# Mixture-of-experts stage: values gathered token by token and weighed in four 32-column groups

## The chip, the cores and the metric

The kernel runs on one core of a Trainium2 chip. The metric is the device time in microseconds (us), here the median of three runs.

## The reference, cut to what matters

One decoder layer, for 1024 prompt tokens and 32 sample tokens. The change touches only its channel mixer, `peer`, in which every token picks 16 of 16384 experts in each of 8 heads (128 slots a token), and every expert is a key row and a value row of 1024 float32 (4 KB each):

```
def block(xb):                                   # 128 tokens
    q = (xb @ w_pq).reshape(PEER_BLOCK, PEER_HEADS, 2, HALF_KEY)
    s = einsum('thpd,pnd->thpn', q, sub_keys)
    sv, si = top_k(s, TOPK)                      # 16 of 128, twice a head
    comb, cidx = sums and numbers of all 256 pairs
    tv, ti = top_k(comb, TOPK)
    eidx = take_along_axis(cidx, ti, axis=-1)
    g = softmax(tv, axis=-1)
    ue, ve = exp_u[eidx], exp_v[eidx]
    a = gelu(einsum('td,thkd->thk', xb, ue))
    return einsum('thk,thkd->td', g * a, ve)
```

## The kernel before, in words

`program` (L1964) runs stage after stage: attention and convolution for both groups of tokens, `merge`, the output product, then `key_weights` (L1378), `experts` (L1486) and the last product. Every stage is a block in which each engine runs its own instruction stream in order, and semaphores alone tie the streams together. All data is float32, and `hT` keeps the residual in SBUF, 128 channels by tokens.

`experts` goes through 8 tiles of 128 prompt tokens and a last tile of the 32 sample tokens, which is folded four times over the 128 partitions, so that it has 2 heads and not 8. A unit is one head of one tile: 66 units. The work of a unit:

- TensorE `score` (L1574): 8 matmuls of 128x256 give the scores of both halves of a key; ScalarE `take_scores` (L1646) copies them to SBUF.
- VectorE `pick` (L1709 to L1754): top 16 of each half, 70 candidate sums, top 16 of these, and the 16 expert numbers (a loop of 16 small operations, L1750). ScalarE `gates` (L1651) takes the exponentials.
- GpSimd `head` (L1536): a copy of the unit's 16 numbers (L1538), then 16 indirect gathers of keys and 16 of values (both L1545). A gather brings one row of 4 KB to each of the 128 partitions, that is for one slot of all 128 tokens, into a ring of 8 buffers `U` or 8 buffers `V`. From the ninth on, a gather waits until its buffer is free.
- VectorE `dot` (L1794, the dot products at L1798): token times key row, one operation a gather, which frees the U buffer.
- ScalarE `weights` (L1657): Gelu of the 16 dots (L1659); VectorE multiplies with the gate (L1802); ScalarE builds for each slot a diagonal matrix of the 128 weights (L1665, ring of 4).
- TensorE `weigh` (L1583): diagonal times V buffer, two matmuls of 128x512 a gather (L1589), added up in PSUM over all slots of the tile. This frees the V buffer.

Picks run a whole tile ahead: `pick` of tile t+1 is interleaved with the dots of tile t, and `advance_indices` (L1756) and `advance` (L1768) pass the finished tile on. So VectorE does 8 picks, then a ninth, before the first dot. In the steady loop VectorE's order is pick(n+8), dot(n); TensorE's is score(n+9), weigh(n); GpSimd's is keys of n, values of n. The loops are hardware loops (`Fori`), and `hold` (L72) is a wait followed by an increment of a counter that nothing reads.

```
L1821-1822  pick(PH * t + PH + h, h)
            dot(PH * t + h, ds(h * TOPK, TOPK))
L1620-1621  score(t + 1, PH * t + PH + h + 1, h + 1)
            weigh(PH * t + h)
```

One other place matters for comparison: sample attention's weighing (L999) runs its matmuls on 32 columns each, four column groups in turn.

Of the kernel before, what the change touches and what calls it, by code (L numbers as in the profile page):

```python
# [7 lines left out]
I32 = mybir.dt.int32  # L8
# [4 lines left out]
ds = bass.ds  # L13
# [1472 lines left out]
def experts(nc, sh, io, wk):  # L1486
    NU, NV, ND = 8, 8, 4
    U0, V0, G0 = NU, NV + TOPK, 1
    NC_ = 70

    blocks = [(0, 2, 16), (2, 8, 5), (8, 16, 1)]
    with Scope(nc, "exp") as s:
        ust = s.sb("ust", [P, KD, P])
        xbn, xb = s.sb("x_next", [P, D]), s.sb("x", [P, D])
        sc = s.sb("scores", [P, 2 * PH, P])
        s1, s2 = s.sb("s1", [P, 2, P]), s.sb("s2", [P, 2, P])
# [4 lines left out]
        tv, ti, tif, ntv = s.sb("tv", [P, TOPK]), s.sb("ti", [P, TOPK], U32), s.sb("tif", [P, TOPK]), s.sb("ntv", [P, 1])  # L1501
        picked, ef = s.sb("picked", [P, TOPK, NC_]), s.sb("ef", [P, TOPK])
        idx_next, idx_cur = s.sb("idx_next", [P, SLOTS], I32), s.sb("idx_cur", [P, SLOTS], I32)
        idx_now = s.sb("idx_now", [P, 2, TOPK], I32)
        ge, gsum, grec, gate = s.sb("ge", [P, SLOTS]), s.sb("gsum", [P, PH]), s.sb("grec", [P, PH]), s.sb("gate", [P, SLOTS])
        dots, act_dots, wt = s.sb("dots", [P, TOPK]), s.sb("act_dots", [P, TOPK]), s.sb("wt", [P, TOPK])
        U, V = s.sb("U", [P, NU, D]), s.sb("V", [P, NV, D])
        diag = s.sb("diag", [P, ND, P])
        fold = s.sb("fold", [P, P])
        ysb = s.sb("y", [P, D])  # L1510
        scb = s.ps("sc")
        xt = [s.ps(f"x{i}") for i in range(2)]
        yb = [s.ps(f"y{i}") for i in range(2)]
        names = ("stage_loaded sc_ready sc_copied xb_turned xb_copied tv_ready gate_done "
                 "idx_ready advanced staged u_free v_free gelu_done w_ready diag_ready y_ready y_copied y_turned y_added "
                 "chain adv iota_made fold_zeroed fold_made passed_p passed_a passed_v passed_t passed_s")
# [3 lines left out]
        HS = SLOTS // REP // TOPK  # L1520

        @block.sync
        def _(sp):
            sp.dma_start(ust[:, :, :], sh.u_s[0]).then_inc(e["stage_loaded"], 16)
            with sp.Fori(1, NT + 1) as t:
                hold(sp, e["sc_ready"], PH * t, e["passed_s"])
                hold(sp, e["xb_turned"], 2 * t, e["passed_s"])
                sp.dma_start(ust[:, :, :], sh.u_s[ds(t, 1)].rearrange("a p m n -> p (a m) n")).then_inc(e["stage_loaded"], 16)

        @block.gpsimd  # L1530
        def _(pool):
            pool.iota(iota[:, :], [[1, NC_]], base=0, channel_multiplier=0, allow_small_or_imprecise_dtypes=True)\
                .then_inc(e["iota_made"], 1)
            pool.memset(fold[:, :], 0.0).then_inc(e["fold_zeroed"], 1)

            def head(n, col, hh):  # L1536
                hold(pool, e["v_free"], V0 + TOPK * (n - 1), e["passed_p"])
                pool.tensor_copy(idx_now[:, hh, :], idx_cur[:, col]).then_inc(e["staged"], 1)  # L1538
                hold(pool, e["staged"], n + 1, e["passed_p"])
                for table, buf, ring, free, first, size in ((io["exp_u"], U, u_in, e["u_free"], U0, NU),  # L1540
                                                            (io["exp_v"], V, v_in, e["v_free"], V0, NV)):
                    for k in range(TOPK):
                        if k % 2 == 0:
                            hold(pool, free, TOPK * n + k + 1 + first - size + 1, e["passed_p"])
                        pool.indirect_dma_start(buf[:, k % size, :], None, table[0],  # L1545
                                                bass.IndirectOffsetOnAxis(idx_now[:, hh, k:k + 1], 0))\
                            .then_inc(ring[k % size], 16)
            with pool.Fori(0, NT) as t:
                hold(pool, e["idx_ready"], t + 1, e["passed_p"])
                with pool.Fori(0, PH // 2) as h2:  # L1550
                    for hh in range(2):
                        head(PH * t + 2 * h2 + hh, ds((2 * h2 + hh) * TOPK, TOPK), hh)
            pool.wait_ge(e["idx_ready"], NT + 1)
            for hh in range(HS):
                head(PH * NT + hh, slice(hh * TOPK, (hh + 1) * TOPK), hh % 2)

        @block.tensor
        def _(pe):
            pe.sem_inc(e["v_free"], V0)
            pe.sem_inc(e["y_copied"], 1)  # L1560
            pe.sem_inc(e["y_turned"], 2)
            pe.sem_inc(e["y_added"], 2)
            pe.sem_inc(e["sc_copied"], 1)

            def turn_tokens(t):

                pe.wait_ge(e["stage_loaded"], 16 * t + 16)
                pe.wait_ge(e["y_added"], 2 if isinstance(t, int) and t == 0 else 2 * t)
# [5 lines left out]
            def score(t, q, h):  # L1574

                pe.wait_ge(e["stage_loaded"], 16 * t + 16)
                pe.wait_ge(e["sc_copied"], q + 1)
                for k in range(KD):
                    last = pe.matmul(scb[:, 0:2 * P].rearrange("p (a n) -> p a n", n=P), ust[:, k, :], wk[:, k, ds(2 * h, 2), :],  # L1579
                                     start=k == 0, stop=k == KD - 1)  # L1580
                last.then_inc(e["sc_ready"], 1)

            def weigh(n):  # L1583
                for k in range(TOPK):
                    g = TOPK * n + k
                    pe.wait_ge(e["diag_ready"], G0 + g + 1)
                    pe.wait_ge(v_in[k % NV], 16 * ((TOPK // NV) * n + k // NV + 1))
                    for f in range(2):
                        last = pe.matmul(yb[f][:, :], diag[:, k % ND, :], V[:, k % NV, f * 512:(f + 1) * 512],  # L1589
                                         start=False, stop=False, skip_group_check=True)  # L1590
                    last.then_inc(e["v_free"], 1)

            def begin(t):
                pe.wait_ge(e["y_copied"], t + 1)
                for f in range(2):
                    pe.matmul(yb[f][:, :], sh.zeros[:, 0:P], sh.zeros[:, :], start=True, stop=False, skip_group_check=True)

            def end(t):
                for f in range(2):
                    last = pe.matmul(yb[f][:, :], sh.zeros[:, 0:P], sh.zeros[:, :], start=False, stop=True, skip_group_check=True)  # L1600
                last.then_inc(e["y_ready"], 1)
                pe.wait_ge(e["y_copied"], t + 2)
# [5 lines left out]

            turn_tokens(0)
            with pe.Fori(0, PH) as h:  # L1610
                score(0, h, h)
            score(1, PH, 0)
            def tile(t, last):
                begin(t)
                score(t + 1, PH * t + PH + 1, 1)
                weigh(PH * t)
                pe.wait_ge(e["xb_copied"], 2 * t + 2)
                turn_tokens(t + 1)
                with pe.Fori(1, PH - 1) as h:
                    score(t + 1, PH * t + PH + h + 1, h + 1)  # L1620
                    weigh(PH * t + h)
                if not last:
                    score(t + 2, PH * t + 2 * PH, 0)
                weigh(PH * t + PH - 1)
                pe.wait_ge(e["xb_copied"], 2 * t + 4)
                end(t)
            with pe.Fori(0, NT - 1) as t:
                tile(t, False)
            tile(NT - 1, True)
            begin(NT)  # L1630
            for hh in range(HS):
                weigh(PH * NT + hh)
            end(NT)

        @block.scalar
        def _(act):
            act.sem_inc(e["gate_done"], 1)
            act.sem_inc(e["diag_ready"], G0)
            act.sem_inc(e["gelu_done"], 1)

            def take_tokens(t):
                for f in range(2):
                    act.wait_ge(e["xb_turned"], 2 * t + f + 1)
                    act.activation(xbn[:, f * 512:(f + 1) * 512], xt[f][:, :], ACT.Copy).then_inc(e["xb_copied"], 1)

            def take_scores(q, h):  # L1646
                hold(act, e["sc_ready"], q + 1, e["passed_a"])
                act.activation(sc[:, ds(2 * h, 2), :], scb[:, 0:2 * P].rearrange("p (m n) -> p m n", n=P), ACT.Copy)\  # L1648
                    .then_inc(e["sc_copied"], 1)

            def gates(q, h):  # L1651

                hold(act, e["tv_ready"], q + 1, e["passed_a"])
# [400 lines left out]
```

## Time and profile before

| | |
|---|---|
| median of 3 runs | 5637.24 us (5636.52 to 5650.34) |
| the profiled execution | span 5638.5 us; its own time is not listed apart from the runs |
| busy shares | TensorE 68%, VectorE 48%, GpSimd 47%, ScalarE 18% |
| DMA | 1331.83 MB, mean 236 GB/s |
| expert stage | from about 1905 us to 5396 us of the span |

The profile is a record of one execution. Times in it are microseconds from the first instruction (ns where marked). PE is TensorE's matmuls and PEld its weight loads, DVE is VectorE, ACT ScalarE, POOL GpSimd. A float32 matmul shows as two records. A name such as exp_V<-in_exp_v is what is written and what it is read from; the bracket behind a row of the timeline is the engine's idle time before it and what ended it.

### The profile page before, as it was taken

Reading aid. Unit: us, or ns where it says so; the run is one execution under the profiler, and the core shown is the slowest. Engines: PE = TensorE matmul, PEld = TensorE weight load, DVE = VectorE, ACT = ScalarE, POOL = GpSimd, SP = SyncE. Lnnn points to the kernel's source line nnn. Section 1 sums busy time; section 2 is a strip of 40 time slices with the busy share of each in tenths; the row PEclk is TensorE's granted clock in tenths of the full one; section 3 lists DMA queues with packets and bytes.
Section 4 is the critical chain, followed back from the end, with each engine's and each line's share of the span. In section 5 each row is a group of like instructions: output and inputs, shape, how many; then the busy total and the mean of one; then the engine's idle time right before and its main releaser. Section 6 shows DMA issues by size and latency. Waiting matters only on the chain. (4 is left out here: it accounts for less than half of the span.)

```text
span 5638.5 us, 57052 instructions
## 1 busy us (share of the span) xinstructions
PE 3830.5 (68%) x14101; PEld 2341.2 (42%) x14101; DVE 2710.5 (48%) x8425; ACT 1038.5 (18%) x2091; POOL 2646.9 (47%) x2596
## 2 busy tenths in 40 slices
PE   6799854554997656676666666766666666766667
PEld 6667831322887523333333333333333333333246
DVE  2233275343112566555655565555555555555433
ACT  2122121111001211122121121121112111121121
POOL 2100222222112056666666666666666666666621
PEclk8855977777998777887888888888888878888879
DMA  2200166663112379999999999999999999999921
GB/s 62 73 23 12 37 227 221 225 237 106 57 46 61 98 253 331 333 327 323 333 331 325 331 328 332 328 327 335 333 324 328 325 329 329 330 328 333 329 90 50
DMA packets 471328, 1331.83 MB, mean 236 GB/s; under 512 B 48641, under 2 KB 141259, under 8 KB 471257
## 3 DMA queue, kind: packets, MB, share of 16 engines
q0 software_dynamic: 326240, 1180.32, 58.3%
q1 hardware_dynamic: 145024, 150.76, 8.7%
q8 instruction: 28, 0.46, 0.0%
q14 instruction: 36, 0.29, 0.0%
HBM read 1307.67 MB, written 23.66 MB: 236 GB/s over the span
## 5 line engine op out<-in xcount | busy, mean ns | idle before, releaser
L1589 PE MATMUL exp_ps_y<-exp_V,exp_diag 128*128 128x512 f32 x4224 | 1978.3, 632 | 1144.0 <-ACT exp_diag L1665 1125.5
L1798 DVE CUSTOM_DVE_ANT_0 exp_U<-exp_U,exp_x 128x1024 f32<-128x1024 f32 x1056 | 1294.4, 1226 | 1179.8 <-DMA exp_U<-in_exp_u,exp_idx_now 1154.9
L1589 PEld LDWEIGHTS exp_ps_y<-exp_V,exp_diag 128*128 128x128 f32 x4224 | 854.2, 204 | 2241.2 <-issue 1925.2
L1545 POOL DMA_INDIRECT exp_V<-in_exp_v,exp_idx_now x1056 | 1055.4, 999 | 735.5 <-PE exp_ps_y L1589 514.0
L1545 POOL DMA_INDIRECT exp_U<-in_exp_u,exp_idx_now x1056 | 1190.4, 1127 | 383.0 <-issue 312.2
L1665 ACT ACTIVATE exp_diag<-all_ident,exp_wt 128x128 f32<-128x128 f32 x1024 | 389.9, 398 | 1186.4 <-PE exp_ps_y L1589 1137.1
L1579 PE MATMUL exp_ps_sc<-ffn_wk,exp_ust 128*128 (+1 forms) x1152 | 276.4, 395 | 36.1 <-ACT exp_scores L1648 36.1
L1659 ACT ACTIVATE exp_act_dots<-exp_dots 128x16 f32<-128x16 f32 x66 | 14.2, 216 | 1384.4 <-DVE exp_dots L1798 1384.4
L1579 PEld LDWEIGHTS exp_ps_sc<-ffn_wk,exp_ust 128*128 128x128 f32 x1152 | 228.0, 199 | 96.6 <-issue 58.0
L1750 DVE SCALAR_TENSOR_TENSOR exp_picked<-exp_iota,exp_tif,exp_cidx 128x70 f32<-128x70 f32 x1152 | 252.8, 290 | 2.6
L999 PE MATMUL satt_ps_o<-satt_pages,satt_kT 128*32 128x512 f32 x512 | 92.8, 889 | 199.7 <-DMA satt_pages<-in_cache_v 197.5
L898 POOL DMA_DIRECT2D satt_pages<-in_cache_v x128 | 69.0, 539 | 249.6 <-issue 244.3
L958 PE MATMUL satt_ps_t<-all_ident,satt_pages 128*128 128x128 f32 x1024 | 130.0, 284 | 75.5 <-DMA satt_pages<-in_cache_k 37.8
L958 PEld LDWEIGHTS satt_ps_t<-all_ident,satt_pages 128*128 128x128 f32 x1024 | 117.0, 147 | 117.1 <-issue 53.6
L854 DVE SCALAR_TENSOR_TENSOR heads_yT<-convin_gp,all_wdw,heads_yT 128x1024 f32<-128x1024 f32 x120 | 153.3, 1278 | 0.0
L414 PE MATMUL merge_ps_b<-merge_x_high,merge_w_high 128*128 128x352 f32 x384 | 128.5, 335 | 28.8 <-POOL merge_w_low L366 28.8
L898 POOL DMA_DIRECT2D satt_pages<-in_cache_k x128 | 69.8, 546 | 165.6 <-issue 160.5
L655 PE MATMUL patt_ps_s<-patt_kh,patt_qh 66*128 66x512 f32 (+2 forms) x192 | 131.5, 823 | 20.8 <-DMA patt_kh<-k_rows 20.8
L364 POOL CAST merge_w_high<-merge_w 128x1024 fp32r<-128x1024 f32 x16 | 20.6, 1285 | 265.8 <-DMA merge_w<-in_w_in 265.8
L1137 POOL MEMSET convin_gp<- 128x120 f32 x1 | 0.2, 203 | 303.5 <-POOLq L116 303.5
L999 PEld LDWEIGHTS satt_ps_o<-satt_pages,satt_kT 128*32 128x32 f32 x512 | 23.9, 161 | 258.6 <-issue 258.6
L415 PE MATMUL merge_ps_b<-merge_x_low,merge_w_high 128*128 128x352 f32 x384 | 123.6, 322 | 0.0
(309 smaller groups left out, 5107.0 us busy)
## 6 DMA issues: line engine op xcount, KB each, us to landing
satt_pages<-in_cache_k SPq DMA_DIRECT2D x128, 256.0 KB, 4.1
satt_pages<-in_cache_k POOLq DMA_DIRECT2D x128, 256.0 KB, 4.3
satt_pages<-in_cache_v SPq DMA_DIRECT2D x128, 256.0 KB, 6.3
satt_pages<-in_cache_v POOLq DMA_DIRECT2D x128, 256.0 KB, 6.4
exp_U<-in_exp_u,exp_idx_now POOLq DMA_INDIRECT x1056, 6.1
exp_V<-in_exp_v,exp_idx_now POOLq DMA_INDIRECT x1056, 5.6
merge_w<-in_w_in SPq DMA_DIRECT2D x16, 512.0 KB, 4.0
keys_w<-in_w_pq SPq DMA_DIRECT2D x16, 512.0 KB, 4.9
```

What stands on the lines that cost most here:

```text
L414: pe.matmul(self.bank(j, c), w_high, x_high, start=first, stop=False)
L415: pe.matmul(self.bank(j, c), w_high, x_low, start=False, stop=False)
L655: last = pe.matmul(sbank[n % 2][:, c0:c1], qh[:, b, qb * P:(qb + 1) * P], kh[:, b, c0:c1], start=True, stop=True)
L854: ins = dve.scalar_tensor_tensor(out=y, in0=x, scalar=wc, in1=y, op0=ALU.mult, op1=ALU.add)
L898: eng.dma_start(ring[:, b, p, :], cache[0, ds(page, 1)].rearrange("a k h d -> k (a h d)"))\
L958: last = pe.transpose(tb[c][:, p * P:(p + 1) * P], ring[:, b, p, c * P:(c + 1) * P], sh.ident[:, :])
L1545: pool.indirect_dma_start(buf[:, k % size, :], None, table[0], bass.IndirectOffsetOnAxis(idx_now[:, hh, k:k + 1], 0))\
L1579: last = pe.matmul(scb[:, 0:2 * P].rearrange("p (a n) -> p a n", n=P), ust[:, k, :], wk[:, k, ds(2 * h, 2), :], start=k == 0, stop=k == KD ...
L1589: last = pe.matmul(yb[f][:, :], diag[:, k % ND, :], V[:, k % NV, f * 512:(f + 1) * 512], start=False, stop=False, skip_group_check=True)
L1665: act.activation(diag[:, k % ND, :], ident[:, :], ACT.Copy, scale=wt[:, k:k + 1]).then_inc(e["diag_ready"], 1)
L1750: st.did(dve.scalar_tensor_tensor(out=picked[:, k, :], in0=iota[:, :], scalar=tif[:, k:k + 1], in1=cidx[:, :], op0=ALU.is_equal, op1=ALU.mult,
L1798: dve.tensor_tensor_reduce(out=row, in0=row, in1=xb[:, :], scale=1.0, scalar=0.0, op0=ALU.mult, op1=ALU.add, accum_out=dots[:, k:k + 1]).t ...
```

## The change

Units and their work stay, but the order changes and the code is written out without loops.

- The values are gathered by token: a gather brings the 128 value rows of one token (all heads and slots), slot by slot over the partitions. For this the expert numbers of a tile are transposed by TensorE (`turn_indices`) and copied to `idxT` by VectorE (`take_indices`), and so are the weights (`turn_weights`). ScalarE writes them into `spread` (`spread_weights`), a matrix of zeros in which column m of a 32-column block holds token m's 128 weights.
- `weigh` handles four tokens at once: for each half of the 1024 channels, four matmuls of 32 columns, each into its own 32 partitions of the PSUM bank. No diagonals are built any more.
- Values begin LAG = 136 gathers behind the keys. GpSimd issues in tick n the 16 keys of unit n, then values 16n-136 to 16n-121. There are 75 ticks of GpSimd and 76 of the other engines; the last 8.5 have values alone.
- `pick` runs two units ahead (LEAD = 2), not a tile, straight from the score buffer of which there are now two; the copy at L1714 is dropped.

The core of the diff:

```diff
-            def head(n, col, hh):
-                hold(pool, e["v_free"], V0 + TOPK * (n - 1), e["passed_p"])
-                pool.tensor_copy(idx_now[:, hh, :], idx_cur[:, col]).then_inc(e["staged"], 1)
...
+            def gather_u(n, k):
+                r = TOPK * n + k
+                if k == 0:
+                    pool.wait_ge(e["idx_ready"], n + 1)
+                if r >= NU:
+                    pool.wait_ge(e["u_free"], r - NU + 1)
...
+            def gather_v(v):
+                t, j = min(v // P, NT), v - P * min(v // P, NT)
+                if j == 0:
+                    pool.wait_ge(e["idxT_ready"], t + 1)
+                if v >= NV:
+                    pool.wait_ge(e["v_free"], v - NV + 1)
+                each = NS if t < NT else NS // 4
+                token = each * (j % 4) + j // 4
+                pool.indirect_dma_start(V[:, v % NV, :], None, io["exp_v"][0],
+                                        bass.IndirectOffsetOnAxis(idxT[:, t % 2, token:token + 1], 0))\
+                    .then_inc(v_in[v % NV], 16)
+
+            for n in range(NTICK):
+                if n < NUNIT:
                     for k in range(TOPK):
+                        gather_u(n, k)
+                for v in range(max(0, TOPK * n - LAG), min(NTOK, TOPK * (n + 1) - LAG)):
+                    gather_v(v)
...
+            def weigh(v):
+                t, m = min(v // P, NT), (v - P * min(v // P, NT)) // 4
+                final = m == (NS if t < NT else NS // 4) - 1
+                for g in range(4):
+                    pe.wait_ge(v_in[(v + g) % NV], 16 * ((v + g) // NV) + 16)
...
+                for f in range(2):
+                    for g in range(4):
+                        x = pe.matmul(yb[t % 2][f][g * NS:(g + 1) * NS, :], spread4[:, g, m, :], V[:, (v + g) % NV, f * 512:(f + 1) * 512],
+                                      start=m == 0, stop=final, skip_group_check=True)
+                        if f == 1:
+                            x.then_inc(e["v_free"], 1)
...
+            for n in range(NTICK + 1):
+                if n + LEAD < NUNIT:
+                    if tile_of(n + LEAD) != tile_of(n + LEAD - 1):
+                        turn_tokens(tile_of(n + LEAD))
+                    score(n + LEAD)
...
+                for k in range(TOPK):
+                    v = TOPK * n + k - LAG
+                    if 0 <= v < NTOK:
+                        if v % P == 0:
+                            turn_weights(v // P)
+                        if v % 4 == 3:
+                            weigh(v - 3)
...
+            def take_scores(n):
+                act.wait_ge(e["sc_ready"], n + 1)
+                if n >= 2:
+                    act.wait_ge(e["sc_read"], n - 1)
...
+            for n in range(NTICK + 1):
+                if n + LEAD < NUNIT:
...
+                    take_scores(n + LEAD)
+                if 1 <= n <= NUNIT:
+                    gelu(n - 1)
+                if n + LEAD < NUNIT:
+                    gates(n + LEAD)
...
+            def pick(n):
+                t, h = tile_of(n), n - PH * tile_of(n)
+                src, b = sc[:, n % 2, :, :], n % 2
+                dve.wait_ge(e["sc_copied"], n + 1)
...
+            def dot(n):
+                t = tile_of(n)
+                dve.wait_ge(e["xb_copied"], 2 * t + 2)
                 for k in range(TOPK):
+                    r = TOPK * n + k
+                    dve.wait_ge(u_in[r % NU], 16 * (r // NU) + 16)
...
+            def weights(n):
+                t, h = tile_of(n), n - PH * tile_of(n)
+                dve.wait_ge(e["gate_done"], n + 1)
+                st.link(dve.reciprocal(grec[:, n % 4:n % 4 + 1], gsum[:, n % 4:n % 4 + 1]))
+                dve.wait_ge(e["gelu_done"], n + 1)
...
+            for n in range(LEAD):
+                pick(n)
+            for n in range(NTICK + 1):
+                if n + LEAD < NUNIT:
+                    pick(n + LEAD)
+                if 1 <= n <= NUNIT:
+                    weights(n - 1)
...
+                if n < NUNIT:
+                    dot(n)
```

## Rows read from the trace of the kernel before

**Rows 1.** The page's span and engine busy times.

```profile
span 5638.5 us, 57052 instructions
PE 3830.5 (68%) x14101; PEld 2341.2 (42%) x14101; DVE 2710.5 (48%) x8425; ACT 1038.5 (18%) x2091; POOL 2646.9 (47%) x2596
```

**Rows 2.** Windows: length, busy PE, PEld, DVE, ACT, POOL, clock, DMA share, GB/s.

```profile
2500.00:3500.00 1000.00, 673.94 (x1629) 322.24 (x1628) 564.04 (x1979) 193.01 (x441) 665.31 (x644) 0.83 0.91 327
```

**Rows 3.** Windows of 4 us inside two units.

```profile
3016.00:3020.00 4.00, 4.00 (x11) 1.85 (x10) 3.41 (x33) 0.80 (x2) 2.41 (x3) 1.00 0.52 157
...
3048.00:3052.00 4.00, 0.00 (x0) 0.00 (x0) 3.45 (x5) 0.00 (x0) 3.09 (x4) 0.50 1.00 395
```

**Rows 4.** Waits, 2500 to 5300 us: total, times, longest.

```profile
DVE exp_U L1798 <- DMA exp_U<-in_exp_u,exp_idx_now: 969.8, 435, 24.2
...
POOL exp_V L1545 <- PE exp_ps_y L1589: 420.4, 275, 6.4
```

**Rows 5.** Timeline of GpSimd over one unit: start, duration, instruction.

```profile
3029.79 0.97 POOL L1545 DMA_INDIRECT exp_U<-in_exp_u,exp_idx_now  x1 [0.99 <-POOL exp_idx_now L1538]
...
3040.78 1.06 POOL L1545 DMA_INDIRECT exp_U<-in_exp_u,exp_idx_now  x1 [0.30 <-issue]
...
3051.91 1.10 POOL L1545 DMA_INDIRECT exp_V<-in_exp_v,exp_idx_now  x1 [0.30 <-issue]
...
3060.91 0.94 POOL L1545 DMA_INDIRECT exp_V<-in_exp_v,exp_idx_now  x1 [0.30 <-issue]
3066.39 0.94 POOL L1545 DMA_INDIRECT exp_V<-in_exp_v,exp_idx_now  x1 [4.54 <-PE exp_ps_y L1589]
...
3080.07 0.97 POOL L1545 DMA_INDIRECT exp_U<-in_exp_u,exp_idx_now  x1 [0.98 <-POOL exp_idx_now L1538]
```

**Rows 6.** The page's DMA issues: count, median us to landing.

```profile
exp_U<-in_exp_u,exp_idx_now POOLq DMA_INDIRECT x1056, 6.1
exp_V<-in_exp_v,exp_idx_now POOLq DMA_INDIRECT x1056, 5.6
```

**Rows 7.** Timeline of GpSimd, first unit, from the ninth key gather.

```profile
2016.43 1.15 POOL L1545 DMA_INDIRECT exp_U<-in_exp_u,exp_idx_now  x1 [2.49 <-DVE exp_dots L1798]
2017.88 1.99 POOL L1545 DMA_INDIRECT exp_U<-in_exp_u,exp_idx_now  x1 [0.30 <-issue]
...
2030.90 0.94 POOL L1545 DMA_INDIRECT exp_V<-in_exp_v,exp_idx_now  x1 [0.30 <-issue]
```

**Rows 8.** Timeline of VectorE, first unit, first and last of 16 dots.

```profile
2013.24 1.23 DVE L1798 CUSTOM_DVE_ANT_0 exp_U<-exp_U,exp_x 128x1024 f32<-128x1024 f32 x1
...
2035.41 1.23 DVE L1798 CUSTOM_DVE_ANT_0 exp_U<-exp_U,exp_x 128x1024 f32<-128x1024 f32 x1
```

**Rows 9.** Sample attention's weighing on 32 columns, and a window with its clock.

```profile
1204.19 5.54 PE L999 MATMUL satt_ps_o<-satt_pages,satt_kT 128*32 128x512 f32 x32 [14.87 <-DMA satt_pages<-in_cache_v]
...
1208.00:1209.00 1.00, 1.00 (x12) 0.33 (x8) 0.00 (x0) 0.00 (x0) 0.00 (x0) 0.97 0.00 0
```

**Rows 10.** Timeline of TensorE: two scores.

```profile
1958.20 5.40 PE L1579 MATMUL exp_ps_sc<-ffn_wk,exp_ust 128*128 x16 [4.56 <-ACT exp_scores L1648]
...
1998.33 3.72 PE L1579 MATMUL exp_ps_sc<-ffn_wk,exp_ust 128*128 128x256 f32 x16 [1.74 <-ACT exp_scores L1648]
```

**Rows 11.** Timeline of ScalarE: score copy in the loop and behind it.

```profile
1987.67 1.28 ACT L1648 ACT_TABLE_LOAD   x1
...
1997.91 0.36 ACT L1648 ACTIVATE exp_scores<-exp_ps_sc 128x256 f32<-128x256 f32 x1
```

**Rows 12.** Timeline of VectorE: a pick from its first to its last operation.

```profile
1992.17 0.29 DVE L1714 COPY exp_s<-exp_scores 128x256 f32 x1 [1.05 <-DVE exp_idx_next L1754]
...
2001.38 0.17 DVE L1754 CAST exp_idx_next<-exp_ef 128x16 f32 x1
```

**Rows 13.** Timeline of VectorE: first dot of the unit of rows 5.

```profile
3035.00 1.23 DVE L1798 CUSTOM_DVE_ANT_0 exp_U<-exp_U,exp_x 128x1024 f32<-128x1024 f32 x1 [15.44 <-DMA exp_U<-in_exp_u,exp_idx_now]
```

**Rows 14.** Timeline of VectorE: last operation of the expert stage.

```profile
5395.36 0.73 DVE L1808 TENSOR_TENSOR all_hT<-exp_ps_x,all_hT 128x128 f32<-128x128 f32 x2 [34.37 <-PE exp_ps_x L1605]
```

More of the change, by code:

```diff
@@ L1548, in _ @@
[L1548 to L1555, printed above, removed]
+            pool.memset(spread[:, :, :], 0.0).then_inc(e["spread_zeroed"], 1)
@@ L1572, in turn_tokens, with score @@
                     last.then_inc(e["xb_turned"], 1)
-            def score(t, q, h):
+            def score(n):
+                t = tile_of(n)
                 pe.wait_ge(e["stage_loaded"], 16 * t + 16)
[L1577 to L1580, printed above, removed]
-                last.then_inc(e["sc_ready"], 1)
@@ L1583, in weigh @@
[L1583 to L1591, printed above, removed]
@@ L1593, in begin @@
-            def begin(t):
-                pe.wait_ge(e["y_copied"], t + 1)
[L1595 to L1602, printed above, removed]
+                if n >= 1:
+                    pe.wait_ge(e["sc_copied"], n)
@@ new lines, in score @@
+                if t < NT:
+                    h = n - PH * t
+                    for k in range(KD):
+                        last = pe.matmul(scb[:, 0:2 * P].rearrange("p (a n) -> p a n", n=P), ust[:, k, :], wk[:, k, 2 * h:2 * h + 2, :],
+                                         start=k == 0, stop=k == KD - 1)
+                else:
+                    for k in range(KD):
+                        for r in range(4):
+                            h = 2 * r + n - PH * NT
+                            last = pe.matmul(scb[r * NS:(r + 1) * NS, 0:2 * P].rearrange("p (a n) -> p a n", n=P),
+                                             ust[:, k, 0:NS], wk[:, k, 2 * h:2 * h + 2, :], start=k == 0, stop=k == KD - 1)
@@ L1609, in _ @@
             turn_tokens(0)
[L1610 to L1633, printed above, removed]
+            for n in range(LEAD):
+                score(n)
+            for n in range(NTICK + 1):
[3 more added lines that the diff above has]
+                    score(n + LEAD)
+                for t in range(NT + 1):
+                    if n == last_unit(t):
+                        turn_indices(t)
+                    if n == y_tick(t):
+                        turn_sums(t)
+                for k in range(TOPK):
[5 more added lines that the diff above has]
+                            weigh(v - 3)
@@ L1732, in pick @@
                     at += na * nb
-                for dst, first, second in ((cand, sv[:, 0, :], sv[:, 1, :]), (cidx, sbase[:, :], sif[:, 1, :])):
+                for dst, one, two in ((cand, sv[:, 0, :], sv[:, 1, :]), (cidx, sbase[:, :], sif[:, 1, :])):
                     if dst is cidx:
@@ L1827, in _ @@
[L1827 to L1837 removed]
+                    y = xt[f][:, :].rearrange("p (k n) -> p k n", n=P)
```

339 lines of the change are left out of this document (159 added, 180 removed).

## The prediction, made before the changed kernel ran

> **What bounds the kernel now.** The span is 5638.5 us, and no engine is busy for more than 68% of it [rows 1]. Nothing lies between span and metric: the median of the three runs is 5637.24 us, so I sum against the span. The change touches only `experts`, so I look at its steady part. There DMA works at a share of 0.91 and 327 GB/s with TensorE at 674 us of 1000 and GpSimd at 665 [rows 2]. GpSimd runs 33 instructions a unit (one head of one tile: 16 key gathers, 16 value gathers, one copy), so 644 of them in 1000 us are 19.5 units, 51.2 us each. Is DMA the limit? No: in the same loop it moves 395 GB/s in one 4 us window and 157 in another, where GpSimd had issued nothing [rows 3]. The waits say why: GpSimd waits 420 us for the V buffers that TensorE frees, and VectorE 970 us for keys [rows 4]. One unit in order of time [rows 5]: U0 at 3029.79, U8 at 3040.78, V0 at 3051.91, V7 at 3060.91, a pause of 4.54 us for TensorE, V8 at 3066.39, the next U0 at 3080.07. So the bound is a ring: dots, Gelu, diagonals, weighing, V buffer, gather, next keys, dots. It closes in 50 to 51 us. The question is what ring the changed program closes.
>
> **Removed.** Values no longer wait for this unit's dots (they are 136 gathers late), so the diagonals go from ScalarE, and the index copy of GpSimd (0.2 us and about 1 us of waiting a unit). Eight picks ahead of the first gather become two: VectorE does 3 picks before its first dot, not 9. Bytes are the same: 1056 gathers of keys and of values, 512 KB each [rows 6]. One matmul pair per gather stays, but on 32 columns, so four gathers may share the array.
>
> **Added: a new ring.** Read the orders. VectorE, tick n: pick(n+2), weights(n-1), dot(n). Pick(n+2) needs score(n+2). TensorE does score(n+2) first in tick n, that is behind weighing all values of tick n-1. GpSimd issues those behind the 16 keys of n-1, of which the last eight wait for dots of n-1. And keys U8 of tick n wait for dot(n), which stands behind pick(n+2). So each tick is serial: dots, rest of keys, all 16 values, their landing, weighing, score, copy, pick, dots. Before, picking lay beside weighing and cost nothing; its cover is gone. Behind the waiting VectorE are queued its dots, and behind them GpSimd.
>
> The tick, from S, the start of its first dot:
> 1. U8 is issued when one dot (1.23 us) is over, 0.8 us later (after the second dot's end at about 2015.6 comes the issue at 2016.43 [rows 7, 8]): S+2.05. Eight gathers on to V0 took 11.1 us between dots that waited for keys [rows 5] and 14.5 us beside dots back to back [rows 7]. In the new tick eight keys lie ready, which is nearer the second; I take 13.0: V0 at S+15.0.
> 2. V3 is issued 3.9 us later (9.0 us for seven gathers [rows 5]) and lands 6.1 us after that, the median of keys [rows 6], since it follows a burst: S+25.0.
> 3. Weighing four. No row of `exp` shows 32 columns; sample attention's do: 16 matmuls of 128x512 on four column groups took 5.54 us, about 3.8 at clock 0.5 (1.2 GHz), the rest at full (2.4) [rows 9]: 8.6 thousand cycles, so eight take 3.6 us at 1.2 GHz, 1.8 at 2.4. The clock rose there after some 3.8 us of unbroken work, and here TensorE pauses between groups: 3.6. V8 waits for it: 28.6, plus 0.8: S+29.4, 4 us later than GpSimd could.
> 4. V7 lands at 15.0+9.0+6.1 = 30.1 and is weighed at 33.7; V12 goes at S+34.5, V15 at S+38.3. It lands 5.6 us later, the median of values [rows 6], 43.9, and is weighed at S+47.5.
> 5. Score: 5.40 us where the clock starts low, 3.72 where it is full [rows 10]; it follows 3.6 us of work, so 4.5: S+52.0.
> 6. ScalarE's copy, 0.36 us and 0.45 of signals. In the loop a table load of 1.28 us precedes it, but right behind an Exp in straight code none does [rows 11], and the new code is straight: 0, bound 1.28. S+52.8.
> 7. Pick: 9.38 us from its first copy to the index cast [rows 12], less that copy (0.33): 9.05. Weights: two small operations, 0.5. S+62.35.
> 8. Per tile, token transposes and copies (2 us), indices (0.3), sums (1.4) and the change of weights on TensorE (2): 5.7 of eight ticks, 0.7 each. **The tick is 63.0 us.**
> The next U0 to U7 go at S+39.6 to 48.6, hidden.
>
> The DMA page of the Trainium skill (DMA: Bandwidth & Descriptors, "Anatomy of one DMA") fits a gather as 2.0 us plus bytes over 436 GB/s, 3.2 us for 512 KB. A key gather issued at 3029.79 let its dot start at 3035.00, 5.2 us later [rows 5, 13], so the trace does not agree. By the page's figure, in both landings of the tick, it would be 57.7 us, and the total some 290 us less.
>
> **The sum.** The first dot is at 2013.24 [rows 8]; six picks of 10.4 us (9.38 and 1.05 between [rows 12]) fewer put it at 1951. Ticks 0 to 7 have no values: 23.4 us of dots (2013.24 to 2036.64 [rows 8]), 9.05 and 0.5: 264, so 2215. Tick 8 has eight values and the first spread: 50.6, so 2265. Ticks 9 to 62 close the ring 54 times: 3402, so 5667. Two more ticks pick nothing: V15, next key 1.3, landing 5.2: 44.8 each, 5757. V0 of the last follows 17 us later. From there 152 values are alone: eight of them per 3.8+5.6+3.6+0.8 = 13.8 us, 262, so 6036. Sums and transposes 4: 6040. Before, the last addition ended at 5396.1 [rows 14]. So +644: **6282 us**. The loss is 54 x (63.0 - 51.2) = 637 and 262 for the tail of values; the earlier start and the ticks without values or picks bring part of it back.
>
> Bounds of the tick: V0 at S+13.15, all weighing and the score at full clock, landing 5.2: 56.3 us, total 5890. V0 at 16.55, both landings 6.1 or more, score 5.4, table load 1.28, tile work twice: 67.9, total 6546. Fetching unrolled code has no row; nothing, or on the path up to 1 us a tick, 54.
>
> **Rivals.**
> A, faster. Some wait of the ring is met early (the score ready before the values, say by another order than I read), so that GpSimd sets the pace: 665 us busy and 644 gaps of 0.30 us are 858 us per 19.5 units [rows 2, 5], 44 us, plus 4 us for V8: 48. That is 15 us x 54 less: 5472. Speaks for it: DMA and GpSimd have that room. Against it: the orders are written out. It decides below a tick of 51.1 us (63.0 - 644/54).
> B, the column groups do not overlap, the change not doing what it says: eight matmuls then take four times the cycles, 7.3 us at full clock. The values end at S+59.0, the tick is 73.8, the total 6935. Against it: sample attention's 5.54 us.
> C, everything at its low bound, the clock staying full from group to group: 5890. For it: the clock is 1.00 during weighing now [rows 3]; against it: the gaps of about 4 us between groups.
> D, dots hold GpSimd off. Beside dense dots gathers took 1.99 us and not 0.94, but three or four of eight [rows 7]. If all eight did, V0 comes at S+20.4 and the total is 6574. The Trainium skill's overview (Trainium Architecture — The Big Picture, "What this means for kernel authors") says that VectorE and GpSimd share a port pair by an exclusive lock; the trace agrees in part, as the 0.94 us gathers beside dots show.
> E, nothing measurable: gain and loss cancel at a tick of 51.1.
>
> **Numbers.** My sum 0.76, A 0.06, B 0.06, C 0.05, D 0.05, E 0.02. Leaving out A, B, C and E (0.19) the range is 5990 to 6590: the bounds, cut a little below, where four terms must all be low, and with D above. Faster by over 0.3% (about what a measurement of this kernel can tell) is A, 0.06; within it E, 0.02; slower all else, 0.92.
>
> **What would show it.** Right: VectorE idle before each pick, released by ScalarE's scores; GpSimd pausing before U8 by some 12 us, released by dots; ticks of 63 us; DMA down to about 265 GB/s; TensorE mostly at low clock in weighing; a tail of 250 us with values alone. Step 3 is wrong if V8 waits for nothing or for 8 us; step 1 if V0 follows U8 by 11 or by 18. The forecast falls if the picks' idle time is short, that is, if scores lie ready when the dots end.

## The result, and the profile after

| | median | runs | span of the profiled execution |
|---|---|---|---|
| before | 5640.24 us | 4 | 5638.5 us |
| after | 6398.07 us | 4 | 6390.4 us |

The ratio is 1.134, with an interval of 1.131 to 1.137: 13% slower. The forecast was 6282 us.

The page's span and busy times of the changed kernel, against [rows 1]:

```profile
span 6390.4 us, 48298 instructions
## 1 busy us (share of the span) xinstructions
PE 2683.4 (42%) x14061; PEld 1636.1 (26%) x14061; DVE 2566.8 (40%) x7980; ACT 629.5 (10%) x1018; POOL 2838.7 (44%) x2530
```

TensorE's busy time fell by 1147 us and ScalarE's by 409, and the kernel became slower: the work of these engines was not what bounded it.

Windows of the changed kernel in the steady part and in the tail (length, busy PE, PEld, DVE, ACT, POOL, clock, DMA share, GB/s), against [rows 2]:

```profile
2500.00:3500.00 1000.00, 249.68 (x1237) 88.06 (x1236) 444.28 (x1618) 61.96 (x106) 569.12 (x490) 0.61 0.73 257
5900.00:6160.00 260.00, 121.78 (x611) 28.75 (x612) 1.97 (x4) 2.29 (x5) 129.34 (x137) 0.68 0.82 287
```

490 gathers of GpSimd in 1000 us are 15.3 units at 32, 65.3 us each, against 51.2 before. DMA went from a share of 0.91 to 0.73. The second row is the tail: VectorE at 2 us of 260, values alone.

Waits of the changed kernel, 2500 to 5500 us (total, times, longest), against [rows 4]:

```profile
PE exp_ps_y L1646 <- DMA exp_V<-in_exp_v,exp_idxT: 2184.0, 180, 41.4
DVE exp_sv L1761 <- ACT exp_scores L1698: 1529.9, 47, 35.5
...
POOL exp_U L1563 <- DVE exp_dots L1814: 688.9, 47, 16.7
```

VectorE used to wait for keys; now it waits before each pick for ScalarE's scores, 47 times 32.6 us. GpSimd waits as often, 14.7 us each, for the dots behind that pick.

One tick in order of time, from the timelines of GpSimd, TensorE, ScalarE and VectorE (start, duration, instruction; in brackets the idle time before it and who ended it). A tick runs from the first dot of one unit to the first dot of the next; S, the start of the first dot, is 3029.29 here:

```profile
3030.79 1.69 POOL L1563 DMA_INDIRECT exp_U<-in_exp_u,exp_idx  x1 [14.24 <-DVE exp_dots L1814]
3032.78 1.98 POOL L1563 DMA_INDIRECT exp_U<-in_exp_u,exp_idx  x1 [0.30 <-issue]
...
3039.65 1.99 POOL L1563 DMA_INDIRECT exp_U<-in_exp_u,exp_idx  x1 [0.30 <-issue]
3041.94 0.94 POOL L1563 DMA_INDIRECT exp_U<-in_exp_u,exp_idx  x1 [0.30 <-issue]
...
3045.69 0.94 POOL L1575 DMA_INDIRECT exp_V<-in_exp_v,exp_idxT  x1 [0.30 <-issue]
...
3056.08 3.42 PE L1646 MATMUL exp_ps_y<-exp_V,exp_spread 128*32 128x512 f32 x16 [37.17 <-DMA exp_V<-in_exp_v,exp_idxT]
3059.74 0.94 POOL L1575 DMA_INDIRECT exp_V<-in_exp_v,exp_idxT  x1 [3.03 <-PE exp_ps_y L1646]
...
3065.54 0.95 POOL L1575 DMA_INDIRECT exp_V<-in_exp_v,exp_idxT  x1 [1.10 <-PE exp_ps_y L1646]
...
3069.30 0.95 POOL L1575 DMA_INDIRECT exp_V<-in_exp_v,exp_idxT  x1 [0.30 <-issue]
3070.55 0.94 POOL L1563 DMA_INDIRECT exp_U<-in_exp_u,exp_idx  x1 [0.30 <-issue]
...
3075.73 3.23 PE L1646 MATMUL exp_ps_y<-exp_V,exp_spread 128*32 128x512 f32 x16 [2.50 <-DMA exp_V<-in_exp_v,exp_idxT]
3078.89 1.43 PE L1596 MATMUL exp_ps_x<-all_ident,exp_ust 128*128 128x128 f32 x8
3080.15 3.62 PE L1607 MATMUL exp_ps_sc<-ffn_wk,exp_ust 128*128 128x256 f32 x16
3083.81 0.38 ACT L1698 ACTIVATE exp_scores<-exp_ps_sc 128x256 f32<-128x256 f32 x1 [0.19 <-PE exp_ps_sc L1607]
3084.22 0.49 DVE L1761 MAX8 exp_sv<-exp_scores 128x8 f32<-128x128 f32 x2 [32.07 <-ACT exp_scores L1698]
...
3093.11 0.17 DVE L1804 CAST exp_idx<-exp_ef 128x16 int32<-128x16 f32 x1
...
3095.04 1.69 POOL L1563 DMA_INDIRECT exp_U<-in_exp_u,exp_idx  x1 [14.80 <-DVE exp_dots L1814]
```

The rows form one chain with no slack. U8, the ninth key gather, is issued at 3030.79 and the first value gather V0 at 3045.69. V8 follows the first group's weighing (3059.74), and V15 goes at 3069.30. Then come the fourth group, a tile's token transposes (in one tick of eight), the score, its copy and the pick, and the next U8 is issued 64.25 us after this one.

### The profile page after: what moved, and what is told of

Same layout as the page of the kernel before. It is cut to its first block and busy times, and to the rows that moved or that the text cites. A ratio compares the mean times of both kernels' runs of the same rounds, so it can differ in the third digit from the quotient of the medians.

```text
span 6390.4 us, 48298 instructions
## 1 busy us (share of the span) xinstructions
PE 2683.4 (42%) x14061; PEld 1636.1 (26%) x14061; DVE 2566.8 (40%) x7980; ACT 629.5 (10%) x1018; POOL 2838.7 (44%) x2530
## 3 DMA queue, kind: packets, MB, share of 16 engines
q0 software_dynamic: 326240, 1180.32, 52.2%
## 5 line engine op out<-in xcount | busy, mean ns | idle before, releaser
L1646 PE MATMUL exp_ps_y<-exp_V,exp_spread 128*32 128x512 f32 x4224 | 854.2, 951 | 2846.0 <-DMA exp_V<-in_exp_v,exp_idxT 2828.6
L1563 POOL DMA_INDIRECT exp_U<-in_exp_u,exp_idx x1056 | 1365.8, 1293 | 1187.9 <-DVE exp_dots L1814 868.1
L1814 DVE CUSTOM_DVE_ANT_0 exp_U<-exp_U,exp_x 128x1024 f32<-128x1024 f32 x1056 | 1245.3, 1222 | 283.8 <-DMA exp_U<-in_exp_u,exp_idx 279.7
L1575 POOL DMA_INDIRECT exp_V<-in_exp_v,exp_idxT x1056 | 1082.4, 1025 | 599.1 <-PE exp_ps_y L1646 313.1
L1646 PEld LDWEIGHTS exp_ps_y<-exp_V,exp_spread 128*32 128x32 f32 x4224 | 170.1, 146 | 3458.5 <-issue 3458.5
L1761 DVE MAX8 exp_sv<-exp_scores 128x8 f32<-128x128 f32 x132 | 32.1, 285 | 1794.8 <-ACT exp_scores L1698 1794.8
L1607 PE MATMUL exp_ps_sc<-ffn_wk,exp_ust 128*128 128x256 f32 x1024 | 268.3, 420 | 169.1 <-ACT exp_scores L1698 110.9
L1698 ACT ACTIVATE exp_scores<-exp_ps_sc 128x256 f32<-128x256 f32 x66 | 25.1, 380 | 2561.9 <-PE exp_ps_sc L1607 1766.9
L1800 DVE SCALAR_TENSOR_TENSOR exp_picked<-exp_iota,exp_tif,exp_cidx 128x70 f32<-128x70 f32 x1056 | 229.7, 289 | 2.3
L958 PEld LDWEIGHTS satt_ps_t<-all_ident,satt_pages 128*128 128x128 f32 x1024 | 117.0, 147 | 115.0 <-issue 52.2
L416 PE MATMUL merge_ps_b<-merge_x_high,merge_w_low 128*128 128x352 f32 x384 | 124.2, 323 | 0.0
```

The lines of the kernel that those rows point to most:

```text
L958: last = pe.transpose(tb[c][:, p * P:(p + 1) * P], ring[:, b, p, c * P:(c + 1) * P], sh.ident[:, :])
L1563: pool.indirect_dma_start(U[:, r % NU, :], None, io["exp_u"][0], bass.IndirectOffsetOnAxis(idx[:, tile_of(n) % 2, h * TOPK + k:h * TOPK + ...
L1575: pool.indirect_dma_start(V[:, v % NV, :], None, io["exp_v"][0], bass.IndirectOffsetOnAxis(idxT[:, t % 2, token:token + 1], 0))\
L1646: x = pe.matmul(yb[t % 2][f][g * NS:(g + 1) * NS, :], spread4[:, g, m, :], V[:, (v + g) % NV, f * 512:(f + 1) * 512], start=m == 0, stop=f ...
L1800: st.did(dve.scalar_tensor_tensor(out=picked[:, k % 4, :], in0=iota[:, :], scalar=tif[:, k:k + 1], in1=cidx[:, :], op0=ALU.is_equal, op1=A ...
L1814: dve.tensor_tensor_reduce(out=row, in0=row, in1=xb[:, t % 2, :], scale=1.0, scalar=0.0, op0=ALU.mult, op1=ALU.add, accum_out=dots[:, n % ...
```

## Experiments

Three explanations were in play, and the expectations partly name them by letter: R, the ring of the forecast, closed at the score; T, that values gathered token by token, by transposed indices, are what costs; P, that TensorE's low clock in weighing is what costs. Ticks are means over ticks 9 to 63, of which the last picks nothing and is short; counted so, the changed kernel's tick is 64.6 us (it is 64.9 over the 54 ticks with a pick, 9 to 62). Places in a tick are counted from its first dot. Where no number of runs is given, the kernel ran once, so differences of some 30 us between such kernels, which single kernels show between their own runs, carry no weight.

### The ring opened at the score

```
+    AHEAD = 3
 TensorE, tick n:  -  score(n + LEAD)      +  score(n + AHEAD)
 ScalarE, tick n:  -  take_scores(n + LEAD), gelu(n-1), gates(n+LEAD)
                   +  gelu(n-1), gates(n+LEAD), take_scores(n + AHEAD)
```

> The changed kernel with one edit: scores are computed three units ahead and not two, so that the score a pick needs is made a tick earlier, and ScalarE copies it behind the tick's gates. The picks stay two ahead. Theory R (the tick is a ring through TensorE: values weighed, then score, copy, pick, dots, and only then the rest of the keys): the pick finds its scores ready when the dots end, GpSimd sets the pace, about 48 us a tick in place of 64.6, so 54 x 16.6 = 900 us less, near 5500 us; VectorE waits for keys and not for scores. Theory T (gathering values by token is what is slow, in GpSimd or in DMA): the tick stays at 60 us or more, the time above 6150. Theory P (what costs is TensorE's low clock in weighing): as T, since weighing is unchanged.

Measured: 5626.85 us (10 runs), ratio to before 0.997 (0.995 to 1.000); tick 50.9. One unit more of scores in hand takes away 771 us, all of the loss, with the same gathers in the same order, and the granted clock of the steady part is 0.63, hardly above the changed kernel's 0.61: R stands, T and P fall as explanations of the loss. The size was missed: 5500 us was expected and the tick is 3 us over the expected 48, and uneven (46.8 to 56.5). The picks are one reason: of 54, 38 had no key gather beside them and took 9.6 us on average, and 16 had and took 21.8. The DMA share came back too (windows of this kernel):

```profile
2500.00:3500.00 1000.00, 329.82 (x1582) 114.80 (x1582) 565.41 (x2017) 77.83 (x133) 663.67 (x622) 0.63 0.90 328
```

### The score three ahead, but inside the tick

Both have the edit above, with `score(n + AHEAD)` behind the third group (k == 11) or the second (k == 7), and ScalarE's copy behind its gates.

> A dose of the same: the score is issued behind the third of the four groups of four values weighed in the tick before, not behind the fourth. Theory R: the third group ends at S+45.3, the score at 49.1, the pick starts at 50.3 and not at 55.4, so each tick is 5.1 us shorter, 54 x 5.1 = 275 us less, about 6120. Theories T and P: no change, 6400.

> The score matmuls of the unit three ahead stand behind the second group of weighing matmuls, and ScalarE copies the scores behind its gates; the picks stay two units ahead. The ring theory in its plain form: the second group ends at S+36.5 in the changed kernel, the score would be done at about S+40.5, the next tick's pick can follow the dots' end at once or at 41.5, and the tick is about 41.5 + 9.5 = 51, time near 5,640 us. The ring theory with the completion signal that reaches ScalarE only when the following weighing group has ended (what the run with the score behind the third group showed): pick at S+45.5 to 46, tick about 55, time near 5,860 us. If the ring were not the cause, the time would stay near 6,398 us.

Measured: 6361.6 us and 6052.91 us; ticks 64.3 and 58.4. Both misses, on the slow side. In the first, the score began at S+45.4 but the pick only at 55.0: from its first matmul to its copy by ScalarE the score lasted 9.0 us, against 4.6 in the changed kernel. In the second, the pick began at S+41.6, as the plain theory had it, but took 16.9 us instead of 9.06. Timelines of VectorE and GpSimd in one such pick of the second kernel:

```profile
3168.07 0.37 DVE L1788 TENSOR_TENSOR exp_cidx<-exp_sbase,exp_sif 128x32 f32<-128x32 f32 x3 [0.18 <-DVE exp_cand L1788]
3171.62 0.23 DVE L1794 MAX8 exp_tv<-exp_cand 128x8 f32<-128x70 f32 x1 [3.19 <-remote]
3175.12 0.09 DVE L1795 MATCH_VALUE_LOAD exp_ti<-exp_tv,exp_cand 128x8 f32 x1 [3.27 <-remote]
...
3163.93 0.94 POOL L1564 DMA_INDIRECT exp_U<-in_exp_u,exp_idx  x1 [0.31 <-issue]
...
3172.70 0.95 POOL L1564 DMA_INDIRECT exp_U<-in_exp_u,exp_idx  x1 [0.30 <-issue]
```

Twice VectorE stands still for over 3 us between two operations of 0.2 us. Meanwhile GpSimd issues the next unit's eight key gathers, one every 1.25 us, right behind the value gathers. The late score of the first kernel lies in the same burst. What the burst does to score and pick is taken up below.

### No transposed indices

```
-  dve.tensor_copy(idxT[:, t % 2, 0:w], tb[:, 0:w])
+  dve.tensor_copy(idxT[:, t % 2, 0:w], idx[:, t % 2, 0:w])
```

The values are then fetched slot by slot, so the sums mix tokens.

> The changed kernel, but the numbers by which values are gathered are not transposed: each gather again brings one slot of all tokens, as before the change, in the same number, size and order of instructions; the sums then mix the values of other tokens. Theory R: same time, 6400, tick 64.6. Theory T: the ticks shrink; if the order were the whole loss, to about 51 us and 5650.

Measured: 6440.74 us, tick 65.0. The ticks did not shrink, so which rows are fetched by one gather does not explain the loss. Of the 43 us over the changed kernel 30 lie ahead of the first dot (1970.1 against 1940.3), where the edit changes nothing.

### Dots ahead of the pick

```
 VectorE, tick n:  -  pick(n + LEAD), weights(n-1), dot(n)
                   +  weights(n-1), dot(n), pick(n + LEAD)
```

> VectorE does the dots of a tick before the pick that runs two units ahead; TensorE, ScalarE and GpSimd keep their orders. Theory R, read closely: the pick leaves the ring but the ring stays closed through ScalarE, whose score copy stands ahead of the Gelu that the weights need, and the weights stand ahead of the dots. So the dots start when copy, Gelu with its table load (1.5 us) and weights (0.5) are over, about S+57.2 in place of 64.6: 54 x 7.4 = 400 us less, near 6000. If only the pick's place mattered: as for three units ahead, 5500. Theory T: no change.

Measured: 5982.02 us, tick 57.5, as expected: the pick is off the ring, and the ring remains closed through ScalarE's copy, Gelu, weights and dots.

### Half the channels in a dot

```
-  row = U[:, r % NU, :]            ... in1=xb[:, t % 2, :]
+  row = U[:, r % NU, 0:D // 2]     ... in1=xb[:, t % 2, 0:D // 2]
```

> The sixteen dots of a unit read 512 of the 1,024 channels, so a dot takes about 0.65 us instead of 1.145 (the output then lacks half of each dot product). Every transfer and every wait stays. If GpSimd's 1.99 us per gather beside dense dots comes from VectorE and GpSimd taking turns dot by dot, the eight ring gathers U8 to U15 take about 1.3 us each, first value gather V0 at S+1.0+8x1.3 = about S+11 to 12, and the tick is 4 to 5 us shorter than 64.7: about 60, time near 6,130 us. If a gather takes 1.99 us whatever VectorE does, V0 stays at about S+15 to 16 and the tick at 63 to 64 (time 6,310 to 6,370 us).

Measured: 6010.68 us, tick 58.4, V0 at S+11.25 where it was 16.9: the tick is shorter by 6.2 us, of which 5.7 are V0's. GpSimd in this kernel, from U8 to V0:

```profile
3039.91 1.15 POOL L1563 DMA_INDIRECT exp_U<-in_exp_u,exp_idx  x1 [14.17 <-DVE exp_dots L1814]
3041.36 0.94 POOL L1563 DMA_INDIRECT exp_U<-in_exp_u,exp_idx  x1 [0.30 <-issue]
...
3050.10 0.94 POOL L1575 DMA_INDIRECT exp_V<-in_exp_v,exp_idxT  x1 [0.30 <-issue]
```

10.2 us for eight, against 14.9 in the changed kernel, with the same bytes. So the gathers of 1.99 us are long because of the dots beside them. They follow each other every 2.29 us, two dots of 1.145, as if each had to wait for a place between two dots. The Trainium skill's overview ("Trainium Architecture — The Big Picture", "What this means for kernel authors") has an exclusive lock on a port pair that VectorE and GpSimd share. The run agrees in that dots hold gathers off; that it is this port no run shows.

How the dots follow each other matters too. In the changed kernel they start every 1.15 us, and 261 of 267 key gathers issued among them took 1.9 us on average. In the kernel before they start every 1.28 us, with a pause of 0.1 us or so between them, and 315 of 355 gathers issued among them took about 1.05 us, one to a dot. So a gather is dear only where the dots leave no gap at all; that the pause is what lets it in is argued from these rows, not tested.

### Key and value gathers in turn

```
-  for k in range(TOPK): gather_u(n, k)
-  for v in ...: gather_v(v)
+  for k in range(TOPK): gather_u(n, k); gather_v(TOPK * n + k - LAG)
```

> The changed kernel, but GpSimd alternates one key gather and one value gather instead of bursts of sixteen; the score stays behind the tick's fourth group. Ring theory: the value gathers no longer start at S+16.9, so the last one of the tick is issued at about S+25.7 (as in the run that was mixed and ahead), landed at 32, weighed at 35.7, scored at 39.6, copied at 40.4, picked at 50: tick 51 to 52 if the pick takes 9 us, time about 5,700 us. With picks stretched to 20 us, as in that run, where GpSimd issues gathers without a pause: tick 60 to 62, time 6,150 to 6,250 us. If the bursts were of no account, 6,398 us.

Measured: 5966.39 us, tick 57.0, between the two forecasts. The values were issued (S+25.9) and weighed (35.8) where expected; score and copy lasted to 45.6 instead of 40.4, and the pick 11.4 us. So in the closed ring the order in turn saves 7.6 us of tick, since values need not wait for the last keys, and would save more if score and pick did not take 5.2 and 2.4 us longer. With the scores ahead and the tile work early as well (the first kernel of the next section, 5526.85 us), the order in turn is worse than bursts:

> As the kernel with the early index turns, but GpSimd alternates one key gather and one value gather over all sixteen steps instead of a burst of each. Theory of pace: GpSimd's 32 gathers are 16x0.94 to 1.99 plus 16x0.94, some 44 us per tick when nothing blocks; value gathers then arrive evenly and the key gathers 8 to 15 wait less for dots, but each blocked key gather also blocks a value gather. Expected tick 46 to 48, time 5,350 to 5,470 us, faster than the kernel before. Rival: the key gathers end only at the tick's end, so that the next unit's dots start late by the landing of 6 us: tick 50 to 52, time 5,570 to 5,690 us.

Measured: 5700.39 us (4 runs), 1.010 (1.008 to 1.012) of before; tick 52.1. The rival came true, a little above its range: the keys end late and the dots last to S+31.8 instead of 21.6. The picks of 20 us were in neither forecast.

### The open ring, tile work early

Added to the first experiment: the index turn of a tile one tick earlier on TensorE, `add_sums` behind `dot(n)` on VectorE; then also `pe.wait_ge(e["sc_ready"], n + AHEAD + 1)` after the score.

> The kernel with scores three units ahead and in bursts (5,627 us), with the index turn of a tile done a tick earlier on TensorE and the sums added behind the dots on VectorE. If the per-tile waits (some 30 us in each of 7 tiles in the trace of that run) are what keeps its tick at a mean of 50.9, the time falls by 60 to 150 us, to 5,480 to 5,570 us. If the irregular ticks come from late score signals alone, it stays at 5,590 to 5,630 us.

> The fastest kernel so far (scores three units ahead, early index turns: 5,526.9 us) with the same wait for the score's completion ahead of the first weighing group. Its trace shows ticks of 47.9 to 52.2 us, the longer ones where the score's copy came only at S+72 to 78; 32 gathers of 512 KB at its 341 to 345 GB/s are 48.6 us per tick. If the late copies make the longer ticks, all ticks come to 48.6, time about 5,500 us. If the transfers alone bound it, 5,520 to 5,530 us.

Measured: 5526.85 us (4 runs), 0.981 (0.977 to 0.985) of before, tick 49.2; and 5504.52 us (4 runs), 0.975 (0.972 to 0.978), tick 48.5, both as expected. Both beat both kernels. Windows of the second:

```profile
2500.00:3500.00 1000.00, 365.75 (x1710) 125.58 (x1710) 592.36 (x2109) 81.22 (x139) 652.52 (x661) 0.63 0.92 348
3500.00:4500.00 1000.00, 343.16 (x1673) 123.12 (x1673) 596.31 (x2071) 80.02 (x136) 644.70 (x658) 0.64 0.92 347
```

32 gathers of 524,288 bytes at 347 GB/s are 48.3 us, the tick: with a DMA share of 0.92 the transfers are now the likeliest bound, though no run took bytes away to show it. Whether the added wait helps by itself is not settled: the two intervals overlap a little. What it changed is in the trace: 19 of 54 picks had key gathers beside them without it and none with it, and the mean pick fell from 13.7 to 9.6 us.

### What makes scores and picks slow

> The kernel with the score behind the third group, and one wait more: after the score TensorE waits for the score's own completion before it goes on to the fourth group of weighing matmuls. In that kernel without the wait (6,361.6 us) the score's signal came 5.7 us after its modelled end, together with those of the fourth group. Theory of late signals (a completion is only told late where 32-column matmuls follow 128-column ones without a pause): with the wait the score ends at S+45.3+3.9 = 49.2 and is told at once, the pick starts at S+50 instead of 55.0, the tick is 59.5 instead of 64.3, time about 6,361 - 54x4.8 = 6,100 us, although a wait was added. Rival: the score itself ends late (it needs the time, because its weights and the matmuls' ends are only modelled): then the wait changes nothing or adds the pause, 6,360 to 6,420 us.

Measured: 6372.61 us (4 runs), tick 64.2, pick at S+55.0. My theory of late signals fell. TensorE now stood idle until the signal, and it came no sooner. Timelines of TensorE and ScalarE in this kernel (the matmuls' ends are modelled; the copy starts on the real signal):

```profile
3124.03 3.64 PE L1647 MATMUL exp_ps_y<-exp_V,exp_spread 128*32 128x512 f32 x16 [6.09 <-DMA exp_V<-in_exp_v,exp_idxT]
3127.61 3.74 PE L1608 MATMUL exp_ps_sc<-ffn_wk,exp_ust 128*128 128x256 f32 x16
3136.76 3.64 PE L1647 MATMUL exp_ps_y<-exp_V,exp_spread 128*32 128x512 f32 x16 [5.41 <-remote]
...
3136.74 0.38 ACT L1704 ACTIVATE exp_scores<-exp_ps_sc 128x256 f32<-128x256 f32 x1 [58.98 <-remote]
```

9.1 us from first matmul to signal. Fetching of the unrolled code is not the cause, as far as the recorded packets show: of 51 scores 19 had no packet of an instruction queue within 5 us ahead of them or during them, and these lasted 8.8 us, the other 32 8.6. The last run takes the key burst away from the score and the pick:

```
-  pool.wait_ge(e["idx_ready"], n + 1)
+  pool.wait_ge(e["idx_ready"], n + 1 if n < 10 else min(n + 3, NUNIT))
```

> The kernel with the score behind the third group and its wait (6,372.6 us), and GpSimd begins a unit's key gathers, from unit 10 on, only when the pick of the unit two ahead has ended; so no key gather is issued while the score or the pick runs. Theory of the burst: what kept that score busy or unreported for 9.1 us (first matmul 3127.61, signal 3136.72, against 3.6 to 4.9 in the changed kernel) was the burst of eight key gathers issued back to back at 1.25 us behind the value gathers, in which the score fell. Without the burst the score lasts 3.7 to 4.5 us, the pick starts at S+50 to 51 instead of 55.0 and ends at S+60; the key gathers start then and land 6 us later: tick 65 to 66.5, time about 6,372 + 54x(65.8-64.2) = 6,420 to 6,500 us. Rival: a score between groups of 32 columns takes 9 us whatever GpSimd does: pick at S+55, key gathers at S+64.3, tick 70 to 71, time about 6,700 us.

Measured: 6450.3 us (4 runs), 1.143 (1.139 to 1.147) of before, tick 65.7, as expected; pick at S+52.2, of 9.06 us. The same two engines:

```profile
3091.70 3.64 PE L1647 MATMUL exp_ps_y<-exp_V,exp_spread 128*32 128x512 f32 x16 [5.39 <-DMA exp_V<-in_exp_v,exp_idxT]
3095.27 1.97 PE L1597 MATMUL exp_ps_x<-all_ident,exp_ust 128*128 128x128 f32 x8
3097.04 3.73 PE L1608 MATMUL exp_ps_sc<-ffn_wk,exp_ust 128*128 128x256 f32 x16
3100.82 1.92 PE L1647 MATMUL exp_ps_y<-exp_V,exp_spread 128*32 128x512 f32 x16
...
3100.80 0.38 ACT L1704 ACTIVATE exp_scores<-exp_ps_sc 128x256 f32<-128x256 f32 x1 [2.93 <-PE exp_ps_sc L1608]
```

The score in the same place, behind the third group, now lasts 3.8 us (mean 4.15 over the scores of the ring's ticks, against 8.65). So the burst of key gathers made the score slow, by its issues or by its transfers: the edit holds both back. It says nothing of the pick, which took 9.06 us in both kernels. The total is a little worse because the keys land after the pick: the run moves the cost, and shows it.

## Why the prediction was right, and where it was off

**The ring.** Predicted and shown. The change cost 758 us, and opening the ring at the score alone gave back 771. Taking the pick out of it gave 416, gathers in turn 432, shorter dots 387, the score behind the second group 345; in all of these the ring stayed closed, with fewer or shorter parts, and the tick stayed at 57 us or more. VectorE's wait before each pick, released by ScalarE, is the row the forecast named. Rival A needed a score ready early; only the experiment made it so. Rival B fell at once: a group of four takes 2.8 to 3.6 us on average, by its place in the tick. E fell with the sum.

**The sum against the trace.** First dot 1940.3 (1951 forecast); ticks 0 to 7 257.6 us (264); tick 8 51.6 (50.6); 54 ticks 3507 (3402), that is 64.9 each for 63.0; two more 101.8 (89.6); from V0 to the last weighing 270.9 (262); end at 6149.5 (6040). 105 of the 109 us are the tick, and the remaining terms cancel within 5, some of them by luck: the start came 11 us early and the ticks without values ran 6 us short, while the two ticks without picks and the tail ran 12 and 9 us long.

**Step 1 was the mis-sized term.** I took 13.0 us for eight keys beside dots, between 11.1 and 14.5. Measured: U8 at S+1.5 and V0 at 16.9, 15.4 us, even over the bound: five of eight gathers take about 2 us, not three or four. U8 itself came 0.35 us behind the first dot, not 0.8. Of rival D, which was 5.4 us a tick dearer, a third came true. The low bound of 11.1 came from dots that waited for keys. Here eight keys lay ready when the tick began, the dots were dense for some 10 us, and only the last three gathers found gaps.

**Steps 2 to 5.** V8 at 31.7 (29.4), V15 at 40.8 (38.3): 2.3 and 2.5 us late, nearly all from step 1. V12 waited for the second group, 1.1 us in the row above. The last group began 6.6 us after V15, not 5.6, but took 2.8 on average, not 3.6: weighed at 50.3 (47.5). TensorE was mostly at its low level, as said: the window's mean clock is 0.61. The score's 4.5 us measured 4.6.

**Steps 6 to 8.** No table load ahead of the copy; the two loads of 1.28 us come behind it, beside the pick. Pick 9.06 (9.05). The pick began at 55.4 (52.8, or 53.5 with the 0.7 of tile work, most of which lies ahead of it), and its 1.9 us of delay are the tick's: 64.9 for 63.0.

**Slips in the sums.** They do not touch the forecast. With the terms it names the low bound of the tick adds up to about 55.5 us, not 56.3. The 5.54 us of step 3 are 8.7 thousand cycles, not 8.6. By steps 3 and 4, rival B's values end nearer S+57.5 than 59.0. The price of up to 1 us a tick for fetching unrolled code stands on no row; the runs show no such cost, as the same straight code with the ring open reached a tick of 48.5 us, below the 51.2 of the loops.

**What came right by luck.** The pick's 9.05 us held because in the closed ring GpSimd issues no key gathers at that time. With value gathers alone beside it the pick would have held too: 9.1 us in the run with the dots first and 9.6 in the fastest kernel. With key gathers beside them the same operations took 11 us (gathers in turn) to 22 us (the 16 picks of the first experiment). The forecast did not see that the ring's slowness protects its own terms, and my expectations for the moved scores failed on it.

## What to carry to other kernels

Where every engine runs a fixed order, write down for each first waiting instruction of a turn what it waits for and what is queued ahead of that; if the chain comes back to itself within one turn, the turn is the sum of its parts, however idle the engines are. Lagging one consumer by a tile does not help when a producer of the next turn (here the score) is queued behind it: run that producer a turn further ahead, which here cost one constant and a later place for ScalarE's copy. Then price a moved piece of work with what will run beside it in its new place, not in the old one.

## What the runs showed of the hardware

- **Key gathers back to back slow a score.** While GpSimd issued eight key gathers at 1.25 us behind value gathers, a score lasted 9 us instead of 4.15 to 4.6. Holding the keys back brought it down to 4.15.
- **Picks are slow beside key gathers, and not beside value gathers alone.** This is read from traces; no edit tested it by itself. In the second kernel of the moved scores a pick took 16.9 us instead of 9.06, and 271 of the 444 us that picks spent beside key gathers (up to 1.3 us from an issue, from 2400 to 5000 us of the span) were pauses of over 0.35 us, beside value gathers alone 0 of 54. In the first experiment 16 picks with key gathers beside them took 21.8 us and 38 without 9.6. The transfer rate is not enough to do it: the picks of the run with the dots first, beside four value gathers and 344 GB/s, took 9.1 us. In the kernel before, beside as many and 300 GB/s, they took 9.6, at most 10.0.
- **What it is about key gathers stays open.** With gathers in turn and scores ahead the pauses stand beside both kinds, 201 of 371 us and 213 of 404, but there the kinds alternate, so it doesn't tell them apart. The slow picks have more gathers in a row beside them as well, and no run varied the number or the pace. The profile names no releaser ("remote").
- **Back-to-back dots and gathers alternate**: a gather takes 0.94 us alone and 1.99 beside dots that start every 1.145 us, in steps of two dots. Beside dots that start every 1.28 us it takes about 1.05.
- **TensorE's ends in the profile are modelled.** A score with a row of 3.74 us was signalled 9.1 us after its start; the start of the engine that waits for it is the safer reading.
